# Two projections with the tokens on partitions, and their RMS norms taken on rows

## The chip, the core and the metric

The kernel runs on one core of one Trainium2 chip. The metric is the device time of one execution in microseconds (us), as the median of several executions. TensorE (PE) multiplies, with its weight loads shown apart (PEld); VectorE (DVE), ScalarE (ACT) and GpSimd (POOL) do the elementwise work; SyncE (SP) issues the loads of the weights from memory.

## The reference, cut to what matters

One sequence of 256 tokens, width 2048, passes a first block and then two more mixers. All is fp32. Of the first block this case is about what stands around w_o and w_down:

```python
def rms_norm(x, g):
    y = x * rsqrt(mean(x * x, axis=-1) + 1e-6)
    return y * g
m = concat([a, p]) @ w_o                      # 2048 x 2048
x = x + rms_norm(m, post_mix_g)
h = rms_norm(x, pre_ffn_g)
up = causal_dwconv(h @ w_up, conv_w, conv_b)  # 2048 x 11264, three taps
y = (gelu(up[..., :5632]) * up[..., 5632:]) @ w_down   # 5632 x 2048
x = x + rms_norm(y, post_ffn_g)
```

The second block begins with products of the token-shifted x: xs = x + (shift(x) - x) * mu, then xs @ a_w_in, a 2048 x 2048 matrix for each of four mu.

## The kernel before

**Precision.** Each fp32 operand is split in two fp32r parts: the high part is a rounded copy (ScalarE), the rest is the difference (VectorE). A product is high x high + rest x high + high x rest.

**Weights.** They come in units of 4 tiles of depth x 256 columns (3 tiles in the third w_down group), 512 KB each. SyncE loads unit u to raw slot u (RAWW, 8 slots) once the unit that held it is done (`unit_done`). ScalarE makes the high part in WHI, a ring of 4 slots (`split_unit`, L1620), once the unit four before it is done; VectorE makes the rest in WLO (L2330). `lo_made` then releases TensorE.

**Products.** In most of the kernel the weights are stationary and the tokens move (`unit`, L876): for each 128x128 weight tile one product with 512 columns (both parts of x, 256 tokens each) and one of the weight's rest with 256. A block is 512 output columns, 8 units, over the whole depth; its results lie with features on partitions, in four PSUM banks ACC. The other form stands in `token_rows` (L964) and `output_rows` (L1563): the tokens are stationary, the weights move, three products of 512 columns for each depth tile and token half, results with tokens on partitions. In the first block only the values and, at the end, w_out of the second mixer have that form.

**Order of the stretch.** w_in, attention and pooling; w_o (4 blocks); norm, residual, next norm's operand; then w_up and w_down in three groups of 16, 16 and 12 tiles of the inner width (GROUPS, L439): `tiles // 2` iterations of w_up, then 4 blocks of w_down whose sums are kept in Y; norm, residual, token shift; a_w_in.

**The norm between two products (before).** `scaled_norm_gemm` (L1005) runs w_o or the last w_down group. Pairs of tiles are evacuated to Y, squared by ScalarE (L1822), and scaled by the gain (L1826). Column sums of the squares are products with ones: `four_sums` within the product after units 15, 23 and 27, `token_sums` behind it; then root, reciprocal, `spread_column`, and filler products that keep TensorE at work (`keep_clock`, L890). `add_pair` (L2433) multiplies and adds two feature tiles to X; `h2_low` (L2561), or `mix_two` and `low_two` (L2677, L2686), make the next operand pair by pair. The next product starts with `first_body` (L901), in order of depth, which waits for the operand pair by pair. Its first 8 weight units are split during the norm (`split_ahead`), from places of their own (`raw_ahead`, L507).

**Order on each engine.** All programs are written out by hand, each engine in order, with semaphores between them.

## Time and profile before

| | us |
|---|---|
| median of 3 executions | 2172.55 (2169.7 to 2172.81) |
| profiled execution, its own time | 2170.59 |
| its span | 2168.8 |
| TensorE busy | 2140.4 (99%) |
| VectorE busy | 1487.4 (69%) |
| ScalarE busy | 1082.0 (50%) |
| mean granted TensorE clock | 0.994 |

The page gives one profiled execution. Busy shares are over the whole span. A matmul's duration in the timeline overlaps the next one's, so the pace of a product is read from start to start.

### The profile page before, as it was taken

How to read it: one execution, taken by the hardware profiler on the slowest of the kernel's cores; microseconds unless marked ns; L12 is line 12 of the kernel's file. 1: busy time of each engine (PE TensorE's matmuls, PEld its weight loads, DVE VectorE, ACT ScalarE, POOL GpSimd, SP SyncE). 2: the span in 40 equal slices, each digit the busy share in tenths (PEclk: the TensorE clock that was granted, in tenths of full speed). 3: DMA queues.
4: the chain of work that ended last, by engine and by line, in shares of the span. 5: the costliest groups of instructions: out<-in, count | busy, mean ns of one | idle time of the engine just before them, and what ended most of it. 6: DMA issues, size and time to landing. Idle time of an engine off the chain costs nothing.

```text
span 2168.8 us, 37737 instructions
## 1 busy us (share of the span) xinstructions
PE 2140.4 (99%) x14518; PEld 1832.7 (85%) x14518; DVE 1487.4 (69%) x2064; ACT 1082.0 (50%) x1529; POOL 85.8 (4%) x75
## 2 busy tenths in 40 slices
PE   9999999999999999999999999999899999999998
PEld 8888888888888888888788888887788888888886
DVE  6656568886488865886895589884676544567656
ACT  6444564444444443445654766544434534456543
POOL 0800000000000000000000000001211000000000
PEclk9999999999999999999999999999999999999999
DMA  9655545665666556555466666653454555654553
GB/s 301 210 160 164 167 146 184 185 192 186 191 186 190 187 190 188 187 183 175 151 189 192 185 180 181 204 169 83 132 166 150 184 184 194 185 155 146 172 197 116
DMA packets 398855, 384.42 MB, mean 177 GB/s; under 512 B 43660, under 2 KB 395460, under 8 KB 397764
## 3 DMA queue, kind: packets, MB, share of 16 engines
q1 hardware_dynamic: 398728, 382.66, 56.9%
q8 instruction: 88, 1.44, 0.3%
q14 instruction: 39, 0.32, 0.1%
HBM read 375.73 MB, written 6.87 MB: 176 GB/s over the span
## 4 chain that ended last, share of the span: by engine, by line
PE 91%; DVE 6%; issue 2%; ACT 1%; DMA 0%; POOL 0%; DVEq 0%; ACTq 0%; POOLq 0%
PE acc L884 44%; PE acc L887 22%; PE acc L915 4%; PE acc L977 2%; PE acc L978 2%; PE acc L979 2%; PE aux L1250 2%; PE acc L918 2%; PE acc L1550 1%; PE acc L1552 1%; PE acc L1551 1%; DVE w_lo L2805 1%; PE aux L1174 1%; DVE w_lo L2332 1%; DVE inverse L2796 0%
## 5 line engine op out<-in xcount | busy, mean ns | idle before, releaser
L2332 DVE TENSOR_TENSOR w_lo<-raw_w,w_hi 128x1024 fp32r<-128x1024 f32 (+1 forms) x576 | 693.6, 1224 | 429.0 <-ACT w_hi L1623 428.0
L1623 ACT ACTIVATE w_hi<-raw_w 128x1024 fp32r<-128x1024 f32 (+1 forms) x576 | 597.0, 1047 | 680.2 <-PE acc L887 541.2
L884 PE MATMUL acc<-h,w_hi 128*128 128x512 f32 x1664 | 525.7, 397 | 0.0
L887 PEld LDWEIGHTS acc<-h,w_lo 128*128 128x128 f32 x1664 | 312.6, 188 | 73.8
L887 PE MATMUL acc<-h,w_lo 128*128 128x256 f32 x1664 | 327.0, 278 | 0.0
L884 PEld LDWEIGHTS acc<-h,w_hi 128*128 128x128 f32 x1664 | 254.5, 189 | 0.8
L884 PE MATMUL acc<-x_split,w_hi 128*128 128x512 f32 x704 | 225.1, 401 | 0.0
L884 PE MATMUL acc<-ff,w_hi 128*128 128x512 f32 x704 | 221.5, 396 | 0.2 <-DVE w_lo L2332 0.2
L884 PE MATMUL acc<-xs_b,w_hi 128*128 128x512 f32 x512 | 162.0, 398 | 1.0 <-DVE w_lo L2805 0.9
L887 PEld LDWEIGHTS acc<-ff,w_lo 128*128 128x128 f32 x704 | 132.3, 188 | 31.3
L887 PEld LDWEIGHTS acc<-x_split,w_lo 128*128 128x128 f32 x704 | 132.2, 188 | 31.2
L2805 DVE TENSOR_TENSOR w_lo<-raw_w,w_hi 128x1024 fp32r<-128x1024 f32 x96 | 116.9, 1220 | 43.3 <-ACT w_hi L2055 42.4
L884 PE MATMUL acc<-xs_a,w_hi 128*128 128x512 f32 x448 | 142.2, 399 | 0.7 <-DVE w_lo L2805 0.7
L887 PE MATMUL acc<-x_split,w_lo 128*128 128x256 f32 x704 | 138.7, 278 | 0.0
L887 PE MATMUL acc<-ff,w_lo 128*128 128x256 f32 x704 | 138.3, 278 | 0.0
L2055 ACT ACTIVATE w_hi<-raw_w 128x1024 fp32r<-128x1024 f32 x96 | 100.7, 1054 | 54.5 <-PE acc L887 45.9
L887 PEld LDWEIGHTS acc<-xs_b,w_lo 128*128 128x128 f32 x512 | 96.2, 188 | 22.7
L884 PEld LDWEIGHTS acc<-x_split,w_hi 128*128 128x128 f32 x704 | 108.1, 189 | 2.5 <-issue 0.8
L884 PEld LDWEIGHTS acc<-ff,w_hi 128*128 128x128 f32 x704 | 107.1, 189 | 1.6 <-issue 0.8
L887 PEld LDWEIGHTS acc<-xs_a,w_lo 128*128 128x128 f32 x448 | 84.2, 188 | 19.9
L887 PE MATMUL acc<-xs_b,w_lo 128*128 128x256 f32 x512 | 100.6, 278 | 0.0
L1707 ACT ACTIVATE fold<-acc 128x512 f32<-128x512 f32 x128 | 74.8, 584 | 31.9 <-PE acc L887 21.8
(439 smaller groups left out, 3132.0 us busy)
## 6 DMA issues: line engine op xcount, KB each, us to landing
raw_w<-in_w_up SPq DMA_DIRECT2D x172, 512.0 KB, 3.5
raw_w<-in_a_w_in SPq DMA_DIRECT2D x124, 512.0 KB, 4.3
raw_w<-in_w_in SPq DMA_DIRECT2D x64, 512.0 KB, 4.0
raw_w<-in_w_down SPq DMA_DIRECT2D x64, 512.0 KB, 3.5
raw_w<-in_b_w_qg SPq DMA_DIRECT2D x64, 512.0 KB, 3.7
raw_w<-in_w_o SPq DMA_DIRECT2D x32, 512.0 KB, 3.5
raw_w<-in_a_w_out SPq DMA_DIRECT2D x32, 512.0 KB, 3.5
raw_w<-in_w_k_shared SPq DMA_DIRECT2D x32, 512.0 KB, 3.6
```

The costliest lines, as they stand in the source:

```text
L884: pe.matmul(ACC[2 * b + f], WHI[:, q if hi is None else hi, k, f * P:(f + 1) * P], op[:, kt, :, :].rearrange("p h t -> p (h t)"), start=fi ...
L887: mm = pe.matmul(ACC[2 * b + f][:, 0:T], WLO[:, slot, k, f * P:(f + 1) * P], op[:, kt, 0, :], start=False, stop=last)
L915: pe.matmul(ACC[2 * b + f], hi(2 * x + b)[:, k, f * P:(f + 1) * P], op[:, kt, :, :].rearrange("p h t -> p (h t)"), start=first, stop=False)
L918: mm = pe.matmul(ACC[2 * b + f][:, 0:T], lo(2 * x + b)[:, k, f * P:(f + 1) * P], op[:, kt, 0, :], start=False, stop=last)
L977: pe.matmul(out, xh, wh[:, :, k, :], start=(kt == 0), stop=False)
L978: pe.matmul(out, xh, wl[:, :, k, :], start=False, stop=False)
L979: mm = pe.matmul(out, xl, wh[:, :, k, :], start=False, stop=(kt == KD - 1))
L1623: act.activation(WHI[:, u % 4, 0:ku, :], RAWW[:, u, 0:ku, :], ACT.Copy).then_inc(hi_made, 1)
L1707: act.activation(FOLD[:, j0:j0 + 2, :], BANKS[:, j0:j0 + 2, T:], ACT.Copy, scale=scale).then_inc(low_half, 1)
L2055: act.activation(WHI[:, n % 4, :, :], RAWW[:, slot, :, :], ACT.Copy).then_inc(hi_made, 1)
L2332: dve.tensor_tensor(WLO[:, u, 0:ku, :], RAWW[:, u, 0:ku, :], WHI[:, u % 4, 0:ku, :].bitcast(F32), ALU.subtract)\
L2805: dve.tensor_tensor(WLO[:, slot_of(n), :, :], RAWW[:, slot_of(n), :, :], WHI[:, n % 4, :, :].bitcast(F32), ALU.subtract)\
```

## The change

w_o and w_down take the form with tokens stationary (`rows_block`), so Y holds token rows: half t_, piece c of 512 features. The squares are summed along a row by ScalarE's accumulator (`rows_squared`), the first three pieces' sums are added by VectorE (`first_squares`), and root, reciprocal and scaling act on a column of one number for each token. In the last block the last two quarters of depth run for token half 0 and then for half 1 (`last_rows_block`), so that half 0 is finished earlier. The scaled rows are turned back by TensorE (`rows_turned_back`) to features on partitions and added to X with the gain (`tile_added`). Half 0 and piece 0 of half 1 are turned behind the product; pieces 1 to 3 of half 1 within the next one, by `midway`, which `first_body` now calls behind the first two depth tiles of quarters 0, 1 and 2 (`if pr == 0 and b == 1 and x < 3`). The last two weight units of the product have high parts in HI2 (`split_last`), and the units split ahead have other places and turns: 0 to 3 before the norm, 4 between the halves, 5 to 7 between pairs. The core of the diff (indented less by eight columns; renamed semaphores and changed counts are left out):

```diff
-    ROOT2, RSTD2, AHEAD2 = (N2[1][:, 0, 0, 2 * k:2 * k + 2] for k in range(3))
+    ROOT2, RSTD2, AHEAD2, FIRST_SQUARES = (N2[1][:, 0, 0, 2 * k:2 * k + 2] for k in range(4))
+    SQUARE_SUMS = N2[1][:, 0, 0, 8:16].rearrange("p (t c) -> p t c", t=2)
+    ROWS = Y.rearrange("p (h a) t -> p h (a t)", h=2)
+    SQUARED = SQY.rearrange("p (h c a) t -> p h c (a t)", h=2, c=4)
...
 def hi_ahead(u):
-    return HI2[:, u] if u < 4 else WHI[:, u - 4]
+    return (HI2, HI2, WHI, WHI, WHI, WHI, HI2, HI2)[u][:, (2, 3, 2, 3, 0, 1, 0, 1)[u]]
...
+def hi_of_rows(x, last=False):
+    return HI2[:, 0:2] if last and x == 3 else WHI[:, 2 * x % 4:2 * x % 4 + 2]
...
+    for i in range(1, 4):
+        weights(1, lambda i_, b: (h["w_o"][0], i * 512 + b * 256), by_depth=512)
     for t0, tiles in GROUPS:
         weights(tiles // 2, lambda i, b: (w_up, i * 256 + (t0 * P + b * FF)), by_depth=256 if t0 == 0 else 0, ahead=0 if t0 == 0 else None)
-        late_depth_weights(lambda i, b: (w_down, b * 256), tiles // 4, t0)
-        weights(3, lambda i, b: (w_down, i * 512 + (512 + b * 256)), ku=tiles // 4, kt0=t0)
+        for i in range(4):
+            weights(1, lambda i_, b: (w_down, i * 512 + b * 256), ku=tiles // 4, kt0=t0, by_depth=512)
...
+                if pr == 0 and b == 1 and x < 3 and midway is not None:
+                    midway(x + 1)
...
-        keep_clock(6)
+    def depth_pass(op, out, x, q, k, ku, halves=(0, 1), last=False):
+        kt = q * ku + k
+        wh, wl = hi_of_rows(x, last)[:, :, k, :], WLO[:, 2 * x:2 * x + 2, k, :]
+        for t_ in halves:
+            xh, xl = (op[:, kt, part_, t_ * P:(t_ + 1) * P] for part_ in range(2))
+            pe.matmul(out[t_], xh, wh, start=(x + k == 0), stop=False)
+            pe.matmul(out[t_], xh, wl, start=False, stop=False)
+            mm = pe.matmul(out[t_], xl, wh, start=False, stop=(x == 3 and k == ku - 1))
+        return mm
+    def rows_block(op, i, ku=KU, depth=(0, 1, 2, 3), gate=None, after={}, quarters_done=4):
+        out = [ACC[2 * (i % 2) + t_] for t_ in range(2)]
+        for x in range(quarters_done):
+            pe.wait_ge(lo_made, seen(lo_made, 2))
+            if x == 0:
+                pe.wait_ge(acc_free, seen(acc_free, 2))
+            for k in range(ku):
+                if gate is not None:
+                    gate(depth[x], k)
+                mm = depth_pass(op, out, x, depth[x], k, ku)
+                if k == ku - 1:
+                    mm.then_inc(unit_done, 2)
+                if (x, k) in after:
+                    after[x, k]()
+        return out
+    def rows_turned_back(w, t_, c):
+        if c < 2:
+            pe.wait_ge(y_scaled, 4 * w + 2 * t_ + c + 1)
+        else:
+            pe.wait_ge(rows_scaled, 4 * w + 2 * t_ + c - 1)
+        if t_:
+            pe.wait_ge(row_pieces, 4 * w + c + 1)
+        for k in range(4):
+            mm = pe.transpose(AUX[c][:, k * P:(k + 1) * P], ROWS[:, t_, 512 * c + k * P:512 * c + (k + 1) * P], IDENT)
+        mm.then_inc(rows_turned, 1)
+    def last_rows_block(op, w, ku):
+        out = rows_block(op, 3, ku, quarters_done=2)
+        for t_ in range(2):
+            for x in (2, 3):
+                if t_ == 0:
+                    pe.wait_ge(lo_made, seen(lo_made, 2))
+                for k in range(ku):
+                    mm = depth_pass(op, out, x, x, k, ku, halves=(t_,), last=True)
+                    if t_ and k == ku - 1:
+                        mm.then_inc(unit_done, 2)
+            if t_ == 0:
+                mm.then_inc(half_done, 1)
+        for c in range(4):
+            rows_turned_back(w, 0, c)
+        keep_clock(1)
+        rows_turned_back(w, 1, 0)
+        seen(sq_ready, 8)
     def post_norm_gemm(op, first, bufs):
...
         pe.wait_ge(lo_made, seen(lo_made))
         unit(A1, n // 4 % 2, n % 4, n % 8)
         beside_unit(n)
-    scaled_norm_gemm(B1, lambda: first_body(B1, [(pool_mix_ready, 8)] * 4 + [(mix_ready, 2 * n + 2) for n in range(4)], depth=DEPTH_W_O,
-                                            after={n: (lambda n=n: beside_unit(32 + n)) for n in range(8)}))
-
+    def mix_gate(q, k):
...
+    for i in (1, 2):
+        rows_block(B1, i)
+    last_rows_block(B1, 0, KU)
+    pe.sem_inc(acc_free, 2)
-    first_body(A2, pairs_of(operand), after={5: x2_sums, 6: lambda: gather(AUX[0], N2[2])}, hi=hi_ahead, lo=lambda u: lo_ahead(0, u))
+    first_body(A2, pairs_of(operand), after={5: x2_sums, 6: lambda: gather(AUX[0], N2[2])}, hi=hi_ahead, lo=lambda u: lo_ahead(0, u),
+               midway=lambda c: rows_turned_back(0, 1, c))
     for n, (t0, tiles) in enumerate(GROUPS):
         gemm(tiles // 2 - (n == 0), A2, [])
+        ku = tiles // 4
+        gated_quarters = quarters(gated_ready, ku)
+        def ff_gate(q, k):
+            if k == 0:
+                pe.wait_ge(*gated_quarters[q])
...
+            rows_block(B2, i, ku)
         if n < len(GROUPS) - 1:
-            late_depth_body(B2, quarters(gated_ready, tiles // 4), tiles // 4)
-            gemm(3, B2, [], ku=tiles // 4)
...
+            rows_block(B2, 3, ku)
+    last_rows_block(B2, 1, ku)
...
-    def squared(i, j0):
-        act.wait_ge(acc_free, seen(acc_free, 0, "tile"))
...
+        act.activation(HI2[:, u - 6, 0:ku, :], RAWW[:, u, 0:ku, :], ACT.Copy).then_inc(hi_made, 1)
+    def rows_squared(i, t_, src):
+        act.activation(SQUARED[:, t_, i, :], src, ACT.Square, accum_out=SQUARE_SUMS[:, t_, i:i + 1]).then_inc(sq_ready, 1)
         seen(sq_ready)
+    def rows_of_block(i, copied=None):
+        act.wait_ge(unit_done, seen(unit_done, 8, "tile"))
+        seen(acc_free, 2, "tile")
+        for t_ in range(2):
+            if copied is None:
+                rows_squared(i, t_, ACC[2 * (i % 2) + t_])
+            else:
+                copied(i, t_)
+    def half_norm(w, t_, squared_last, last_piece):
+        if t_ == 0:
+            act.wait_ge(half_done, w + 1)
+        else:
+            act.wait_ge(unit_done, seen(unit_done, 8, "tile"))
+        squared_last(t_)
+        if t_ == 0:
+            act.wait_ge(var_ready, seen(var_ready))
         act.wait_ge(sq_ready, seen(sq_ready, 0))
-        for k in range(2):
-            kt = 4 * i + j0 + k
...
+        act.activation(ROOT2[:, t_:t_ + 1], SQUARE_SUMS[:, t_, 3:4], ACT.Sqrt, scale=1.0 / D,
+                       bias=FIRST_SQUARES[:, t_:t_ + 1]).then_inc(rstd_ready, 1)
+        act.wait_ge(columns_ready, 2 * w + t_ + 1)
+        for c in (2, 3):
+            act.activation(y_row(t_, c), last_piece(t_) if c == 3 else y_row(t_, c), ACT.Copy,
+                           scale=RSTD2[:, t_:t_ + 1]).then_inc(rows_scaled, 1)
+    def blocks_in_rows(ku, evac, first=1):
+        for i in range(first, 4):
+            for u in range(8):
+                if u == 3:
+                    evac(i - 1)
+                if (i, u) == (3, 4):
+                    act.activation(AHEAD2, ONES[:, 0:2], ACT.Sqrt)
+                if i == 3 and u >= 6:
+                    split_last(u, ku)
+                else:
+                    split_unit(u, ku)
+    blocks_in_rows(KU, rows_of_block)
+    for u in range(4):
+        split_ahead(0, u)
+    for t_ in range(2):
+        if t_:
+            split_ahead(0, 4)
+        half_norm(0, t_, lambda t_: rows_squared(3, t_, ACC[2 + t_]), lambda t_: ACC[2 + t_])
+    seen(acc_free, 2, "tile")
     def x_squared(j):
...
+        if p_ in (2, 4, 6):
+            split_ahead(0, 4 + p_ // 2)
...
+            act.wait_ge(acc_free, seen.total(acc_free, "tile") - 1 + t_)
+            rows_squared(i, t_, y_row(t_, i))
+    def last_sum_squared(t_):
+        act.wait_ge(acc_free, seen(acc_free, 1, "tile"))
+        rows_squared(3, t_, y_row(t_, 3))
     pend = None
     for n, (t0, tiles) in enumerate(GROUPS):
...
+        split(0, ku)
+        pend(lambda: two_splits(4, ku))
+        two_splits(6, ku)
+        evac = (lambda i: rows_of_block(i, copied_rows), rows_left, squared_sums)[n]
+        if n < len(GROUPS) - 1:
+            for i in range(1, 4):
+                for u in range(8):
+                    if u == 3:
+                        evac(i - 1)
+                    split_unit(u, ku)
+            pend = lambda evac=evac: evac(3)
+        else:
+            blocks_in_rows(ku, evac)
+    for u in range(4):
+        split_ahead(1, u)
+    for t_ in range(2):
+        if t_:
+            split_ahead(1, 4)
+        half_norm(1, t_, last_sum_squared, lambda t_: y_row(t_, 3))
     def silu_out(dst):
...
+            if p_ in (3, 5, 7):
+                split_ahead(1, 5 + (p_ - 3) // 2)
...
-
-        y2, x2 = Y[:, 2 * p_:2 * p_ + 2, :], X[:, 2 * p_:2 * p_ + 2, :]
...
+    def split_last(u, ku=KU):
+        dve.wait_ge(hi_made, seen(hi_made))
+        dve.tensor_tensor(WLO[:, u, 0:ku, :], RAWW[:, u, 0:ku, :], HI2[:, u - 6, 0:ku, :].bitcast(F32), ALU.subtract).then_inc(lo_made, 1)
+    def blocks_in_rows(ku, evac, last=True):
+        for i in range(1, 4):
+            for u in range(8):
+                if u == 3:
+                    evac(i - 1)
+                if last and i == 3 and u >= 6:
+                    split_last(u, ku)
+                else:
+                    split_unit(u, ku)
+    def first_squares(sums):
+        dve.wait_ge(sq_ready, sums)
+        link(dve.tensor_reduce(FIRST_SQUARES, SQUARE_SUMS[:, :, 0:3], AX.X, ALU.add))
+        dve.tensor_scalar(FIRST_SQUARES, FIRST_SQUARES, 1.0 / D, NORM_EPS, ALU.mult, ALU.add).then_inc(var_ready, 1)
+    def half_scaled(w, t_):
+        dve.wait_ge(rstd_ready, seen(rstd_ready))
+        dve.reciprocal(RSTD2[:, t_:t_ + 1], ROOT2[:, t_:t_ + 1]).then_inc(columns_ready, 1)
+        dve.wait_ge(columns_ready, 2 * w + t_ + 1)
+        for c in range(2):
+            dve.tensor_scalar(y_row(t_, c), y_row(t_, c), RSTD2[:, t_:t_ + 1], None, ALU.mult).then_inc(y_scaled, 1)
+    def tile_added(kt, t_, gain):
+        g, now = COL[gain] + kt, slice(t_ * P, (t_ + 1) * P)
+        return dve.scalar_tensor_tensor(X[:, kt, now], AUX[kt // 4][:, kt % 4 * P:(kt % 4 + 1) * P], PV[:, g:g + 1], X[:, kt, now],
+                                        ALU.mult, ALU.add)
+    def first_half_added(w, c, gain):
+        dve.wait_ge(rows_turned, 8 * w + c + 1)
+        for k in range(4):
+            ins = tile_added(4 * c + k, 0, gain)
+        ins.then_inc(row_pieces, 1)
+    def pair_added(w, p_, gain):
+        if p_ % 2 == 1 and p_ < 6:
+            first_half_added(w, (p_ + 1) // 2, gain)
+        if p_ % 2 == 0:
+            dve.wait_ge(rows_turned, 8 * w + 4 + p_ // 2 + 1)
+        for k in range(2):
+            ins = tile_added(2 * p_ + k, 1, gain)
+        ins.then_inc(x_ready, 1)
...
-        seen(part_out)
-        split_ahead(which, last)
...
+    def copied_rows(i):
+        seen(unit_done, 8, "tile")
+        for t_ in range(2):
+            dve.wait_ge(sq_ready, 4 + 2 * i + t_ + 1)
+            dve.tensor_copy(y_row(t_, i), ACC[2 * (i % 2) + t_]).then_inc(acc_free, 1)
+        seen(acc_free, 2, "tile")
+        if i == 2:
+            first_squares(4 + 6)
+    blocks_in_rows(KU, copied_rows)
+    seen(unit_done, 8, "tile")
+    for u in range(4):
+        split_ahead(0, u)
+    dve.wait_ge(acc_free, seen(acc_free, 0, "tile"))
+    half_scaled(0, 0)
+    first_half_added(0, 0, "post_mix_g")
+    half_scaled(0, 1)
+    seen(acc_free, 2, "tile")
...
             h2_low(p_ - 1)
-        if p_ == 5:
-            split_ahead(0, 7)
+        if p_ in (1, 4, 6, 8):
+            split_ahead(0, (1, 4, 6, 8).index(p_) + 4)
     partial(AUX[0], N2[2])
...
+    def last_half_sum(t_):
+        if t_ == 0:
+            dve.wait_ge(half_done, 1 + 1)
...
+        else:
+            dve.wait_ge(unit_done, seen(unit_done, 8, "tile"))
+        dve.tensor_tensor(y_row(t_, 3), ACC[2 + t_], y_row(t_, 3), ALU.add).then_inc(acc_free, 1)
+        dve.wait_ge(acc_free, seen(acc_free, 1, "tile"))
     pend = None
     for n, (t0, tiles) in enumerate(GROUPS):
         pend = gemm(tiles // 2, up_evac(t0), pending=pend, keep=True, by_depth=(n == 0), early=2 * (n == 0))
-        pend = gemm(4, joiner(Y) if n == 0 else adder(), pending=pend, ku=tiles // 4, keep=True, by_depth=True)
-    first_groups()
-    last_pair_and_reciprocal(1, (0, 1, 2, 3), (4,), 5)
+        ku = tiles // 4
+        split(0, ku)
+        pend(lambda: two_splits(4, ku))
+        two_splits(6, ku)
+        evac = (rows_of_act, summed_rows, last_sums)[n]
+        blocks_in_rows(ku, evac, last=(n == 2))
+        pend = lambda evac=evac: evac(3)
+    for u in range(4):
+        split_ahead(1, u)
+    last_half_sum(0)
+    half_scaled(1, 0)
+    last_half_sum(1)
+    first_half_added(1, 0, "post_ffn_g")
+    half_scaled(1, 1)
     def shift_diff(i):
...
-        if p_ < 8:
-            add_pair(p_)
         if p_ >= 2:
             low_two(p_ - 2)
+        if p_ < 8:
+            pair_added(1, p_, "post_ffn_g")
         if 1 <= p_ < 9:
             dve.wait_ge(x_ready, 8 + p_)
             mix_two(p_ - 1)
-        if p_ in (5, 7):
-            split_ahead(1, {5: 6, 7: 7}[p_])
+        if p_ in (1, 4, 6, 8):
...
```

## Rows read from the trace of the kernel before

**Rows 1.** The page, part 1: busy us, share and instructions of the engines.

```profile
PE 2140.4 (99%) x14518; PEld 1832.7 (85%) x14518; DVE 1487.4 (69%) x2064; ACT 1082.0 (50%) x1529; POOL 85.8 (4%) x75
```

**Rows 2.** Waits of TensorE, 470 to 1066 us: total, times, longest.

```profile
PE aux L994 <- ACT sq L1824: 0.5, 1, 0.5
...
PE acc L884 <- DVE w_lo L2332: 0.2, 1, 0.2
```

**Rows 3.** TensorE's timeline (start, us, engine line op), 1080 to 1094 us.

```profile
1080.72 0.63 PE L915 MATMUL acc<-xs_a,w_hi 128*128 128x512 f32 x2
...
1091.87 0.63 PE L884 MATMUL acc<-xs_a,w_hi 128*128 128x512 f32 x2
```

**Rows 4.** The chain that ended last (start, us, what), in the last product.

```profile
2069.40 0.87 PE aux L1560 x8
...
2137.38 0.87 PE aux L1560 x8
```

**Rows 5.** The same chain, in the first product: sums of four groups.

```profile
27.74 1.86 PE aux L956 x32
```

**Rows 6.** ScalarE by form, 1000 to 1034 us: count, busy us, mean ns, idle.

```profile
L1623 ACT ACTIVATE w_hi<-raw_w 128x768 fp32r<-128x768 f32 x14 | 11.0, 833 | 2.8 <-PE acc L887 2.8
...
L1824 ACT ACTIVATE sq<-y 128x512 f32<-128x512 f32 x5 | 3.2, 632 | 13.2 <-DVE y L2629 13.2
```

**Rows 7.** By form: VectorE, 1000 to 1034 us; ScalarE's accumulator read, 140 to 220.

```profile
L2332 DVE TENSOR_TENSOR w_lo<-raw_w,w_hi 128x768 fp32r<-128x768 f32 x15 | 13.7, 955 | 13.0 <-ACT w_hi L1623 13.0
L2629 DVE TENSOR_TENSOR y<-acc,y 128x512 f32<-128x512 f32 x3 | 2.1, 692 | 0.3
...
L1786 ACT ACTIVATION_READ_ACCUMULATOR scores<-scores,softmax_stats 128x1 f32 x16 | 3.0, 187 | 0.0
```

**Rows 8.** TensorE's timeline around the norm behind w_o.

```profile
304.77 0.40 PE L887 MATMUL acc<-mix,w_lo 128*128 128x256 f32 x2
...
314.76 0.87 PE L915 MATMUL acc<-h,w_hi_ahead 128*128 128x512 f32 x2
...
339.82 0.63 PE L884 MATMUL acc<-h,w_hi 128*128 128x512 f32 x2
```

**Rows 9.** VectorE by form, 140 to 220 us: an operation of 128 columns on PSUM.

```profile
L2503 DVE SCALAR_TENSOR_TENSOR scores<-aux,rstd_columns,bias 128x128 f32<-128x128 f32 x8 | 2.8, 347 | 0.3 <-PE aux L1100 0.3
```

**Rows 10.** VectorE's timeline in both boundaries: rest of h2, mix, weight split ahead.

```profile
315.01 0.87 DVE L2566 SCALAR_TENSOR_TENSOR h<-x,params,h 128x256 fp32r<-128x256 f32 x2
...
322.15 1.22 DVE L2338 TENSOR_TENSOR w_lo_ahead_b<-raw_w_ahead_b,w_hi 128x1024 fp32r<-128x1024 f32 x1
...
1066.68 0.88 DVE L2682 SCALAR_TENSOR_TENSOR xs_quarter<-x,params,xs_quarter 128x255 f32<-128x255 f32 x2
```

**Rows 11.** TensorE's timeline around the norm behind w_down.

```profile
1056.00 0.50 PE L994 MATMUL aux<-consts,ms 128*128 128x1 f32 x4
...
1066.82 1.22 PE L915 MATMUL acc<-xs_a,w_hi_ahead 128*128 128x512 f32 x2 [3.18 <-DVE xs_a L2688]
```

**Rows 12.** Timelines there of SyncE's issues and of ScalarE.

```profile
1047.06 0.37 SPq L593 DMA_DIRECT2D raw_w<-in_a_w_in  x1
...
1054.33 1.06 ACT L1628 ACTIVATE w_hi_ahead<-raw_w 128x1024 fp32r<-128x1024 f32 x1 [1.41 <-DMA raw_w<-in_a_w_in]
```

**Rows 13.** Timelines there of ScalarE's copy and VectorE's rest of one pair.

```profile
1064.90 0.61 ACT L1938 ACTIVATE xs_a<-xs_quarter 128x512 fp32r<-128x512 f32 x1
...
1066.08 0.69 DVE L2688 TENSOR_TENSOR xs_a<-xs_quarter,xs_a 128x512 fp32r<-128x512 f32 x1
```

**Rows 14.** Stretches: us, then busy us and count of PE, PEld, DVE, ACT, POOL; granted clock; DMA.

```profile
308.00:315.00 7.00, 6.54 (x21) 5.45 (x20) 5.94 (x10) 4.87 (x10) 0.00 (x0) 0.51 0.01 2
...
1063.60:1066.80 3.20, 0.04 (x1) 0.00 (x0) 3.17 (x7) 2.10 (x6) 0.00 (x0) 0.85 0.00 0
1066.80:1072.30 5.50, 5.48 (x17) 4.71 (x18) 5.43 (x11) 3.15 (x7) 0.00 (x0) 0.50 0.01 3
1072.30:1080.00 7.70, 7.70 (x45) 6.67 (x44) 7.63 (x14) 3.74 (x8) 0.00 (x0) 0.98 0.45 136
```

189 lines of the change are left out of this document (61 added, 128 removed).

## The prediction

> **What bounds the kernel now.** I read the page's busy times first: TensorE is busy 2140.4 of 2168.8 us [rows 1], so only time on TensorE, or a wait of TensorE, can move the end. Then the waits of TensorE over the whole feed-forward block: half a microsecond for the sums, 0.2 us for a weight rest [rows 2]; the w_down products run back to back and VectorE and ScalarE are hidden. What remains is (a) the pace of the products, (b) the two stretches in which a norm stands between two products, and (c) what a slower VectorE or ScalarE would newly expose. I take them in this order, against the profiled execution (2170.6 us, span 2168.8). It lies 2 us under the median of 2172.55, inside the spread of the three runs; I do not correct for that.
>
> **(a) Pace of the products.** The kernel already holds both forms. With weights stationary, eight depth tiles of a 512-column block take 1080.72 to 1091.87, 11.15 us, 1.394 us each [rows 3]. With tokens stationary (the last product, w_out of the second mixer) the turned pieces of X come at 2069.40 and 2137.38, three blocks of 16 tiles later [rows 4]: 22.66 us a block, less 0.87 for the eight transposes is 21.79, or 1.362 us a tile. Both stream 3072 columns a tile; eight products become six. Gain 0.032 us a tile. w_o has 64 tiles, w_down 4 x (16 + 16 + 12) = 176, together 240: **-7.6 us**. The squares no longer have their sums taken inside the product: 3 groups in each of the two products, 1.86 us for four such groups [rows 5], so 6 x 0.465 = **-2.8 us**. The order of depth at the start of w_down and of w_o asks for the last quarter at three quarters of the block in both kernels, and the last conv pair and its split end before that, so I cost that at nothing (cover: some 4 us; without it the wait is the overrun itself).
>
> The Trainium skill, "TensorE: Matmul & The Clock Gate", section on the 53.3 and 56 ns, gives about 2.5 ns of fixed cost per matmul when warm. Two products fewer would by that be worth 5 ns a tile, 1.2 us in all instead of 7.6, and the forecast would be 6.4 us later. The two rows speak against it here: they give about 14 ns for each product saved.
>
> **(b) The new chain between evacuation and the next weight split.** In blocks 1 to 3 ScalarE and VectorE split weight unit 2, evacuate the block before, then split unit 3, which TensorE wants one quarter into the block: 5.45 us with 4 tiles a unit, 4.09 us with 3. Unit 2 can't be split before the block starts, since its slot is read until then. With 4 tiles: high part of unit 2 to 1.1 us, evacuation (at worst two squares with their accumulator reads) to 2.5, high part of unit 3 to 3.5, rest to 4.8 us: hidden, 0.6 us to spare. In the third w_down group (3 tiles) the order is high part (0.83), rest (0.96), sums on VectorE (0.69 each), squares of the sums on ScalarE (0.63 plus 0.19 for the accumulator), high part, rest [rows 6, 7]. Added with overlap: rest of unit 2 ends at 1.9, sums at 2.5 and 3.2, squares at 3.35 and 4.05, high part of unit 3 starts there, its rest starts at 4.9 and ends at 5.9. TensorE wants it at 4.1. Wait 1.8 us, three times: **+5.5 us** (bounds 0, if the squares slip behind, and 6). Queued behind the squares on ScalarE is the high part of unit 3, and TensorE waits for its rest.
>
> **(c1) Boundary w_o to w_up.** Now the last w_o product ends at about 305.0, the first behind the norm starts at 314.76, and the next loop at 339.82: 34.8 us [rows 8]. After the change, in us from the end of w_o: the first token half is normed by -0.6 (it ended 5.45 us earlier). TensorE turns its four pieces to 1.8. VectorE adds four tiles of the first piece: a 128x128 scalar-tensor-tensor out of PSUM takes 0.347 [rows 9], back to back about 0.27, so 1.15 us, to 1.8. The second half: square to 1.1, root 1.35, reciprocal 2.0, first piece scaled 2.5, turned 3.3, pair added 3.9, then the other half's second piece and the next pair to 5.6 (1.15 + 0.6), rest of h2 (0.87) to 6.5 [rows 10]. First product at 6.6 instead of 9.8: -3.2. But then the pieces turned inside the product make a loop of two engines: TensorE works two depth tiles (2.79 us), turns piece c of the second half, and its *next* gate is an operand pair that VectorE computes only behind the addition which waits for that turn. So TensorE stands for: landing 0.3, two tiles 0.6, rest 0.87, signal 0.1 = 1.85 us. This happens three times (c = 1, 2, 3), plus 0.9 once where four first-half tiles also fall in, plus 0.95 for the sum of squares of x, whose last square comes later: +7.4. The transposes are 3 x 0.45 = 1.35. TensorE reaches the next loop at 40.0 instead of 34.8: **+5.2 us**.
>
> **(c2) Boundary w_down to a_w_in.** Now 1056.0 to 1066.82, and 1091.87 to the next loop: 35.9 us [rows 3, 11]. Here the raw weights come late already: the fourth landed only at 1054.33, 7.3 us behind its issue [rows 12]. The change frees raw slots 2 and 3 at half of the last block, 8.2 us before its end; at the pace of rows 12 the fourth lands at about -1.5 and is split before half 0 is normed. Then: rest of the fourth +0.7, sum 1.4, square 2.2, scaled 3.5; second half sum 4.1, square 5.5, scaled 6.4, turned 7.2, pair 7.8, second piece and pair 9.5, mix (0.87) 10.4, split ahead (1.22) 11.6, rest (0.69) 12.25 [rows 10, 13]: first product at 12.35 instead of 10.8. Inside the product the loop is longer, because between the addition and the gate lie the mix (0.87), ScalarE's copy (0.61) and the rest (0.69): landing 0.3, tiles 0.6, 0.9, 0.7, 0.7 = 3.25 us at c = 1, and at c = 2 and 3 a weight split (1.22) covers the copy's 0.7 and adds 0.5: 3.75 each. Between them 1.25, 1.2 and 1.3 where the first-half tiles or the last pair are late. Sum of waits 14.6, transposes 1.35. Next loop at 50.7, at full clock, instead of 35.9: **+14.8 us**. Every moved step was counted: four tile adds per piece, two per pair, the splits ahead at 1, 4, 6, 8, and SP's order (0, 1, 4, 2, 5, 3, 6, 7), in which 2 and everything behind it waits for the half block.
>
> **Clock.** In both boundaries the granted clock is at the lower level (1.2 GHz) for some microseconds: 0.51 over 308 to 315, and 0.50 over 1066.8 to 1072.3 after 3.2 us without work; 17 matmuls passed in those 5.5 us, against 45 in the 7.7 us behind them [rows 14]: 3.1 a microsecond against 5.8. The change has fewer filler products (1 for 8) and five stretches of 3 us and more without a product. Bounds: nothing, and lower clock through both products (2.35 us on each of some six to eight pairs of tiles, about +16). I take the first pair of (c2) at the lower clock, +2.35, and 1.1 us behind each of its three long waits, since the pair behind a wait has 1.25 us of slack: **+5.7 us**.
>
> Sum: -7.6 - 2.8 + 5.5 + 5.2 + 14.8 + 5.7 = +20.8, so 2170.6 + 20.8 = **2191.4 us**.
>
> **Rivals.**
> A, the other side (faster): VectorE is not in TensorE's way, because additions run ahead and the gate behind a turned piece is already met. For it: VectorE now needs about 2.1 to 2.7 us a pair against 2.79 of TensorE [rows 10]. Against: in the program's order the rest of pair 1 stands behind the addition of pair 2, which waits for the turn. It decides if that wait costs under about 1 us each. Then: -7.6 - 2.8 - 3.2 + 1.35 + 1.5 + 1.35 = -9.4, or 2161 us (2167 with the wait of (b)).
> B: only (c2) is real; (b) hides and (c1)'s loop is half as long: -10.4 + 2 + 14.8 + 2.4 = +8.8, 2179 us.
> C, the clock: the short stretches of work between waits never bring the higher clock back. Price +16 instead of +5.7: 2202 us. For it: the clock is low after a pause half as long as what I expect. Against: the products of the second mixer's end keep theirs. The Trainium skill, "TensorE: Matmul & The Clock Gate", says in its section on the HAM clock gate that the lower clock is the default and activity releases it. Rows 14 agree as far as they go.
> D: a product saved is worth next to nothing, so that only the columns count and (a) shrinks from 7.6 to 1.2 us: 2198 us. For it: both forms stream 3072 columns a tile. Against: the two rows of (a). It is the rule of the Trainium skill weighed in (a).
>
> **How the numbers follow.** Forecast 0.62, A 0.10, B 0.12, C 0.13, D 0.03. The range 2174 to 2205 takes in B, C, D and the bounds of (b) and of the clock, and leaves out A and a little at the top. About 0.2% (4.3 us) is what a measurement of this kernel can tell from no change. Slower by more: the forecast, C, D and most of B, 0.83; within: the edges of A and B, 0.08; faster: 0.09.
>
> **What the changed profile would show.** (a) w_down blocks of 21.8 us (4 tiles) without waits. (b) three waits of TensorE of about 1.8 us on a weight rest in the third group. (c1) first h2 product 6 to 7 us behind w_o, then waits for the operand h of 1.85 us. (c2) waits for xs_a of 3 to 4 us, three of them, and a lower clock around them. What would make it wrong: waits of TensorE in the two first products under 5 us together, or a block that takes 22.3 us as before.

## The result, and the profile after

| | before | after |
|---|---|---|
| median, us | 2171.63 (2169.7 to 2172.81, 4 executions) | 2195.46 (2193.83 to 2196.85, 4 executions) |
| ratio to before, 95% interval | | 1.0112 (1.0100 to 1.0124) |
| profiled execution, its own time, us | 2170.59 | 2193.83 |
| its span, us | 2168.8 | 2192.1 |

The kernel is 1.1% slower. The forecast was 2191.4 us, in the range 2174 to 2205, and against the profiled execution it said +20.8 us where +23.2 came. How much of that agreement is the sum of right terms, and how much is errors that cancel, is what the rest of this document takes apart.

First the page's busy times of the kernel after, beside [rows 1]:

```profile
PE 2135.0 (97%) x13978; PEld 1813.1 (83%) x13978; DVE 1467.8 (67%) x2082; ACT 1064.0 (49%) x1515; POOL 85.8 (4%) x75
```

TensorE is busy 5.4 us less than before, in a span that is 23.3 us longer. The change did save TensorE work; what it costs is waits and, behind them, time at the lower clock. So the next view is the waits of TensorE (engine, line, what it waited for; us in total, times, longest us) from 200 us to the start of the loop behind the second boundary. They add up to 33 us (the four largest are shown). In the kernel before the same stretch has under 6 us, 3.2 of them one wait for xs_a behind w_down [rows 11], and the feed-forward block has 0.7 us [rows 2]:

```profile
PE acc L920 <- DVE xs_a L2857: 14.1, 4, 4.8
PE acc L920 <- DVE h L2708: 7.9, 5, 3.0
PE aux L1042 <- DVE y L2558: 5.1, 2, 4.4
PE acc L1011 <- DVE w_lo L2430: 5.0, 4, 1.6
```

L920 is the high product inside `first_body`, L1042 the turning of a row piece, L1011 the first product of a depth pass in the rows form. Cut by the places where one stage hands over to the next, the two profiled executions compare like this (each mark is the start of the first product of the stage, or the end of the last):

| stretch, us | before | after | difference | forecast |
|---|---|---|---|---|
| to the end of w_o | 305.00 | 299.75 | -5.25 | -3.4 |
| w_o's end to the next loop | 34.8 | 41.05 | +6.25 | +5.2 |
| from there to w_down's end | 716.2 | 713.9 | -2.3 | -1.5 |
| w_down's end to a_w_in's next loop | 35.9 | 57.0 | +21.1 | +20.5 |
| the rest | 1076.9 | 1080.4 | +3.4 | 0 |
| sum | 2168.8 | 2192.1 | +23.3 | +20.8 |

**(a) The pace.** Timeline of TensorE inside a w_down block (start, duration, engine, line, operation, tiles; the pace is start to start). Eight depth passes, one for each token half of four depth tiles, lie between the two rows:

```profile
820.05 0.39 PE L1011 MATMUL acc<-w_hi,ff 128*128 128x512 f32 x1
...
825.49 0.39 PE L1011 MATMUL acc<-w_hi,ff 128*128 128x512 f32 x1
```

5.44 us for four tiles is 1.360 a tile, against 1.394 with weights stationary [rows 3]. Granted clock 1.00 in both kernels from 340 to 1054 us, so the difference is not the clock.

**(b) The third group.** Two of the waits of the third w_down group; there is one in each of its four blocks, of 0.21, 1.61, 1.61 and 1.60 us:

```profile
991.59 0.50 PE L1011 MATMUL acc<-w_hi,ff 128*128 128x512 f32 x1 [0.21 <-DVE w_lo L2430]
...
1005.74 0.50 PE L1011 MATMUL acc<-w_hi,ff 128*128 128x512 f32 x1 [1.61 <-DVE w_lo L2430]
```

What the wait at 1005.74 ended with is in VectorE's timeline: the rest of that unit, which itself waited for its high part. ScalarE began that part at 1003.86, when the second square was done:

```profile
1004.72 2.70 DVE L2430 TENSOR_TENSOR w_lo<-raw_w,w_hi 128x768 fp32r<-128x768 f32 x3 [1.54 <-ACT w_hi L1678]
```

**(c1) The boundary behind w_o.** The timeline of TensorE, with the waits in brackets [us idle <- who ended it]; the turns (transposes of row pieces) are L1042, the first product of the next loop is L889:

```profile
299.75 1.91 PE L1042 MATMUL aux<-consts,y 128*128 128x128 f32 x16
...
306.49 0.73 PE L920 MATMUL acc<-h,w_hi_ahead 128*128 128x512 f32 x2 [3.04 <-DVE h L2708]
...
313.03 0.74 PE L920 MATMUL acc<-h,w_hi_ahead 128*128 128x512 f32 x2 [1.49 <-DVE h L2708]
...
318.73 0.60 PE L1042 MATMUL aux<-consts,y 128*128 128x128 f32 x4
320.82 0.73 PE L920 MATMUL acc<-h,w_hi 128*128 128x512 f32 x2 [1.49 <-DVE h L2708]
...
324.30 0.73 PE L920 MATMUL acc<-h,w_hi 128*128 128x512 f32 x2 [0.41 <-DVE h L2708]
...
329.29 0.74 PE L920 MATMUL acc<-h,w_hi 128*128 128x512 f32 x2 [1.49 <-DVE h L2708]
...
332.83 1.93 PE L956 MATMUL aux<-sq,consts 128*32 128x256 f32 x32 [0.47 <-ACT sq L1937]
...
340.80 0.63 PE L889 MATMUL acc<-h,w_hi 128*128 128x512 f32 x2
```

The first product starts 6.7 us behind the end of w_o (forecast 6.6, before 9.8 [rows 8]). Behind each turn inside the product stands a wait of 1.49 us for the operand h: four tiles turned at 318.73, done at 319.33, and nothing until 320.82.

**(c2) The boundary behind w_down.** The same view, with the three turns inside the product (1074.58, 1085.55, 1097.87):

```profile
1059.14 3.67 PE L1042 MATMUL aux<-consts,y 128*128 128x128 f32 x16 [4.40 <-DVE y L2558]
...
1063.46 1.06 PE L1042 MATMUL aux<-consts,y 128*128 128x128 f32 x4
1069.30 1.22 PE L920 MATMUL acc<-xs_a,w_hi_ahead 128*128 128x512 f32 x2 [4.78 <-DVE xs_a L2857]
...
1074.58 0.85 PE L1042 MATMUL aux<-consts,y 128*128 128x128 f32 x4
1078.31 1.08 PE L920 MATMUL acc<-xs_a,w_hi_ahead 128*128 128x512 f32 x2 [2.89 <-DVE xs_a L2857]
...
1085.55 0.60 PE L1042 MATMUL aux<-consts,y 128*128 128x128 f32 x4
1089.37 1.22 PE L920 MATMUL acc<-xs_a,w_hi 128*128 128x512 f32 x2 [3.23 <-DVE xs_a L2857]
...
1097.87 0.60 PE L1042 MATMUL aux<-consts,y 128*128 128x128 f32 x4
1101.70 0.73 PE L920 MATMUL acc<-xs_a,w_hi 128*128 128x512 f32 x2 [3.23 <-DVE xs_a L2857]
...
1111.73 0.63 PE L889 MATMUL acc<-xs_a,w_hi 128*128 128x512 f32 x2
```

The 16 turns of the first half start 4.40 us late, at 1059.14; w_down ended at 1054.74. The first product starts 14.6 us behind that (forecast 12.35, before 10.8 [rows 11]). Then 2.89, 3.23 and 3.23 us of wait behind the three turns. Who held the first pieces up stands in two rows of ScalarE's timeline and the first two of VectorE's; the third is its first addition of the second half:

```profile
1054.18 1.06 ACT L1683 ACTIVATE w_hi<-raw_w 128x1024 fp32r<-128x1024 f32 x1 [3.01 <-DMA raw_w<-in_a_w_in]
1057.19 0.63 ACT L1884 ACTIVATE sq<-y 128x512 f32<-128x512 f32 x1 [1.95 <-DVE y L2788]
```
```profile
1055.27 1.22 DVE L2436 TENSOR_TENSOR w_lo<-raw_w,w_hi 128x1024 fp32r<-128x1024 f32 x1 [2.84 <-ACT w_hi L1683]
1056.41 0.68 DVE L2788 TENSOR_TENSOR y<-acc,y 128x512 f32<-128x512 f32 x1
...
1064.56 2.16 DVE L2563 SCALAR_TENSOR_TENSOR x<-aux,params,x 128x128 f32<-128x128 f32 x8 [1.62 <-PE aux L1042]
```

The fourth weight unit of a_w_in was issued at 1047.59 and landed 6.6 us later. ScalarE stood 3.01 us for it, VectorE 2.84 us for ScalarE, and the sum of the first token half (L2788), whose products had ended at 1050.6, stood queued behind it until 1056.41. The second half's first piece was turned at 1063.46, and VectorE added from 1064.56 on.

**The clock.** Windows of the kernel after, from w_down's end to the first product and from there to the next loop (us, busy and instructions of each engine, granted clock, DMA):

```profile
core 0: us, PE busy (x) PEld busy (x) DVE busy (x) ACT busy (x) POOL busy (x), PEclk, DMA share, GB/s
1054.70:1069.30 14.60, 5.42 (x24) 4.69 (x23) 10.33 (x25) 8.41 (x17) 0.00 (x0) 0.73 0.05 16
1069.30:1111.70 42.40, 33.06 (x140) 27.98 (x141) 23.63 (x50) 15.48 (x26) 0.00 (x0) 0.77 0.26 85
```

Before, the whole boundary had a granted clock of 0.90; here it is 0.73 and 0.77, TensorE at its lower level (1.2 GHz) for about half of the time.

### The profile page after: what moved, and what is told of

It is laid out like the page before. It is cut to its first block, busy times and chain, and to the rows that moved or that the text cites. A ratio compares the mean times of both kernels' runs of the same rounds, so it can differ in the third digit from the quotient of the medians.

```text
span 2192.1 us, 36112 instructions
## 1 busy us (share of the span) xinstructions
PE 2135.0 (97%) x13978; PEld 1813.1 (83%) x13978; DVE 1467.8 (67%) x2082; ACT 1064.0 (49%) x1515; POOL 85.8 (4%) x75
## 4 chain that ended last, share of the span: by engine, by line
PE 87%; DVE 8%; ACT 2%; issue 2%; DMA 1%; POOL 0%; SPq 0%; DVEq 0%; ACTq 0%; POOLq 0%
PE acc L889 34%; PE acc L892 17%; PE acc L1011 4%; PE acc L1013 4%; PE acc L1012 4%; PE acc L920 3%; PE acc L977 2%; PE acc L979 2%; PE acc L978 2%; PE aux L1305 2%; PE acc L923 1%; DVE w_lo L2974 1%; PE acc L1605 1%; PE acc L1607 1%; PE acc L1606 1%
## 5 line engine op out<-in xcount | busy, mean ns | idle before, releaser
L1678 ACT ACTIVATE w_hi<-raw_w 128x1024 fp32r<-128x1024 f32 (+1 forms) x572 | 588.9, 1046 | 711.2 <-PE acc L892 412.9
L889 PE MATMUL acc<-h,w_hi 128*128 128x512 f32 x1664 | 525.7, 397 | 0.0
L889 PEld LDWEIGHTS acc<-h,w_hi 128*128 128x128 f32 x1664 | 254.7, 189 | 1.0
L889 PE MATMUL acc<-x_split,w_hi 128*128 128x512 f32 x704 | 225.1, 401 | 0.0
L889 PE MATMUL acc<-xs_b,w_hi 128*128 128x512 f32 x512 | 162.1, 398 | 2.0 <-DVE w_lo L2974 2.0
L889 PE MATMUL acc<-xs_a,w_hi 128*128 128x512 f32 x448 | 142.2, 399 | 0.7 <-DVE w_lo L2974 0.7
L1011 PE MATMUL acc<-w_hi,ff 128*128 128x512 f32 x346 | 135.1, 390 | 5.0 <-DVE w_lo L2430 5.0
L1012 PE MATMUL acc<-w_lo,ff 128*128 128x512 f32 x352 | 137.0, 389 | 0.0
L1013 PE MATMUL acc<-w_hi,ff 128*128 128x512 f32 x346 | 134.6, 389 | 0.0
L889 PEld LDWEIGHTS acc<-x_split,w_hi 128*128 128x128 f32 x704 | 108.2, 189 | 2.4 <-issue 0.8
L892 PE MATMUL acc<-xs_a,w_lo 128*128 128x256 f32 x448 | 88.1, 278 | 0.0
L889 PEld LDWEIGHTS acc<-xs_b,w_hi 128*128 128x128 f32 x512 | 78.0, 189 | 4.6 <-DVE w_lo L2974 2.6
```

What stands on the lines that cost most here:

```text
L889: pe.matmul(ACC[2 * b + f], WHI[:, q if hi is None else hi, k, f * P:(f + 1) * P], op[:, kt, :, :].rearrange("p h t -> p (h t)"), start=fi ...
L892: mm = pe.matmul(ACC[2 * b + f][:, 0:T], WLO[:, slot, k, f * P:(f + 1) * P], op[:, kt, 0, :], start=False, stop=last)
L1011: pe.matmul(out[t_], xh, wh, start=(x + k == 0), stop=False)
L1012: pe.matmul(out[t_], xh, wl, start=False, stop=False)
L1013: mm = pe.matmul(out[t_], xl, wh, start=False, stop=(x == 3 and k == ku - 1))
L1678: act.activation(WHI[:, u % 4, 0:ku, :], RAWW[:, u, 0:ku, :], ACT.Copy).then_inc(hi_made, 1)
```

## The experiments

Two of the theories are told apart by edits of order alone. The loop theory: TensorE's waits inside the first products come from where VectorE's program puts the rest of an operand, and from where the turns stand. Against it: VectorE's load (no order helps), the clock, and the late transfer. Times are compared as ratios to the kernel before on the same chip; stretches are read from the traces.

| kernel | median, us | ratio to before (95%) | w_o's end to next loop | w_down's end to next loop |
|---|---|---|---|---|
| before | 2171.63 | | 34.8 | 35.9 |
| after | 2195.46 | 1.0112 (1.0100 to 1.0124) | 41.1 | 57.0 |
| after, again | 2192.02 | 1.0092 (1.0077 to 1.0107) | 41.9 | 56.2 |
| rests first | 2185.85 | 1.0065 (1.0047 to 1.0082) | 38.3 | 52.8 |
| unit 3 first | 2189.72 | 1.0079 (1.0063 to 1.0096) | | 55.6 |
| norm ahead of unit 4 | 2190.01 | 1.0078 (1.0061 to 1.0095) | | 53.8 |
| eight products | 2200.35 | 1.0124 (1.0106 to 1.0142) | | |
| 12 fillers | 2196.63 | 1.0110 (1.0094 to 1.0125) | | 57.0 |
| 5 fillers | 2192.53 | 1.0095 (1.0080 to 1.0111) | | 52.3 |
| pipelined | 2175.05 | 1.0014 (1.0005 to 1.0023) | 35.6 | 43.3 |
| combined | 2165.15 | 0.9968 (0.9958 to 0.9979) | 33.6 | 40.4 |
| combined, with two steps more | 2166.65 | 0.9973 (0.9964 to 0.9982) | 32.1 | 41.8 |

The kernel after was run twice; its ratios differ by 0.2%, so a single ratio is not trusted here to better than that. The finer readings come from the traces. There the waits that follow from the order of the program have the same length to 0.03 us from run to run (1.49; 2.89, 3.23, 3.23). The wait for the first pieces behind w_down, which hangs on a transfer, does not: 3.6 to 5.1 us in the seven traces with the order of the kernel after at that place. Boundaries that an edit does not touch differ too: the first takes 41.1 to 42.7 us, the second 55.6 to 57.0. So a difference of up to 1.7 us in a whole boundary says nothing by itself.

### The rest of an operand ahead of the addition that waits

```diff
+                if p_ % 2 == 0 and p_ >= 2:
+                    h2_low(p_ - 1)
                 if p_ < 8:
                     pair_added(0, p_, "post_mix_g")
-                if p_ >= 1:
+                if p_ % 2 == 1:
                     h2_low(p_ - 1)
...
```

The second boundary likewise: mix and rest of the odd pair ahead of the even pair's addition, and ScalarE's copies in that order.

> VectorE takes the rest of the odd pair (h2, xs_a) ahead of the addition that waits for the turned piece, in both first products; ScalarE's copies of xs_a follow the same order. Loop theory (the program's order on VectorE makes TensorE wait behind each turned piece): the waits for h (1.49 us three times, 0.41, 0.47 in the kernel after) go below 1 us together, those for xs_a inside the product (2.89, 3.23, 3.23) below 3 us together, since VectorE has 6.4 us of work for every 6.0 us of TensorE there; with the clock held up the time falls by 10 to 17 us from 2195.5, to 2178 to 2186. Rival, VectorE's throughput (it has too much work in these stretches whatever the order): the waits move to the pairs ahead of the turned pieces and keep at least two thirds of their 14.7 us; 2190 to 2196.

Measured: ratio 1.0065, profiled 2185.48 us against 2193.83, in the upper part of the loop theory's range. Its timeline of TensorE in the first boundary:

```profile
311.10 0.60 PE L1042 MATMUL aux<-consts,y 128*128 128x128 f32 x4
311.46 0.71 PE L920 MATMUL acc<-h,w_hi_ahead 128*128 128x512 f32 x2
...
314.74 0.73 PE L920 MATMUL acc<-h,w_hi 128*128 128x512 f32 x2 [0.24 <-DVE h L2713]
...
322.42 0.73 PE L920 MATMUL acc<-h,w_hi 128*128 128x512 f32 x2 [1.37 <-DVE h L2713]
...
330.25 1.93 PE L956 MATMUL aux<-sq,consts 128*32 128x256 f32 x32 [1.54 <-ACT sq L1937]
```

The product behind the turn at 311.10 now starts at 311.46 with no bracket: the three waits of 1.49 us are gone, as the loop theory says. But one pair further on there are new ones, 0.24 and 1.37 us, and 1.54 at the squares. In the second boundary the same: nothing behind the turns, then 1.98, 3.11 and 2.09 us a pair later, where 9.35 us had stood before; 7.2 are left, three quarters, against under 3 expected. Of the 14.7 us of waits 10.3 are left, 70%, which is what the rival said (at least two thirds); the time, 2185.9, is what the loop theory said. So this run did not decide between the two. What it shows is that the first link was real, since the waits behind the turns are gone; the new ones suggested a second link that still hung on the turn: the next even pair cannot be added before its piece is turned, and TensorE turned it only halfway through. The next run tests that.

### Turns one pair earlier, VectorE in step

```diff
                 for x, q in enumerate(depth):
+                    if midway is not None and x < 3:
+                        pe.wait_ge(*gates[2 * x])
+                        midway(x + 1)
...
-                        if pr == 0 and b == 1 and x < 3 and midway is not None:
-                            midway(x + 1)
...
+            for c in range(4):
+                pair_added(0, 2 * c, "post_mix_g")
+                h2_low(2 * c)
+                pair_added(0, 2 * c + 1, "post_mix_g")
+                split_ahead(0, 4 + c)
+                h2_low(2 * c + 1)
...
```

The old loop over the pairs goes. `pair_added` of an even pair now also adds the first half's next piece, so that its bank is free one pair earlier. The second boundary has the same order, with the mixes between, and ScalarE rounds a pair before it scales the next.

> Each piece of the second token half is turned one pair earlier (as soon as the pair before is there), and VectorE goes in step: addition of the even pair, first half of the next piece, rest of the even pair, then the odd pair; in the second boundary ScalarE rounds each pair before it scales the next. Loop theory, refined by the run with the rests first (removing the wait behind the turn left waits of 0.2, 1.4, 1.5 us for h and 2.0, 3.1, 2.1 us for xs_a, since the next addition still hung on the turn): with both links cut the waits inside the first h2 product go below 0.7 us together and those inside the first xs_a product below 3 us; w_o's end to the next loop 34.7 us instead of 41.0, w_down's end to the next loop 46 instead of 57; 2178 us. Rival (VectorE's work of about 27 us between w_down's end and the next loop is the bound whatever the order): the second boundary stays above 52 us, 2184 to 2187 us.

Measured: 2175.05 us, ratio 1.0014; boundaries 35.6 and 43.3 us (34.7 and 46 expected). Once it has begun, the first h2 product has no wait left. The first xs_a product has two, 0.70 and 2.08, where 9.35 us had been:

```profile
1061.51 1.12 PE L1043 MATMUL aux<-consts,y 128*128 128x128 f32 x4 [3.94 <-DVE xs_a L2855]
...
1083.08 0.74 PE L923 MATMUL acc<-xs_a,w_hi_ahead 128*128 128x512 f32 x2 [0.70 <-DVE xs_a L2855]
...
1086.82 1.19 PE L923 MATMUL acc<-xs_a,w_hi_ahead 128*128 128x512 f32 x2 [2.08 <-DVE xs_a L2855]
```

This is the main result, and here the rival (the second boundary above 52 us) is out. Of a loss of 20 to 24 us (by the two ratios of the kernel after), 17 to 21 were the order of instructions on VectorE, ScalarE and TensorE: the same instructions in another order take 19.2 us out of the two boundaries (5.5 and 13.7), counted against the first trace of the kernel after. That includes the time at the lower clock that stood behind the waits.

### The unit that TensorE wants first, ahead of the evacuation

```diff
-            def blocks_in_rows(ku, evac, last=True):
+            def blocks_in_rows(ku, evac, last=True, at=3):
...
-                        if u == 3:
+                        if u == at:
                             evac(i - 1)
...
-                blocks_in_rows(ku, evac, last=(n == 2))
+                blocks_in_rows(ku, evac, last=(n == 2), at=3 + (n == 2))
```

ScalarE's program has the same edit.

> In the third w_down group the weight unit that TensorE wants a quarter into the block is split ahead of the evacuation, its sums and squares. Theory (chain through sums and squares): the 5.0 us that TensorE waits for w_lo in that group go to under 0.5, 2190.5 us. Rival (the two engines have too much work in a block of three-tile units): the wait moves to the next unit, and 2 to 5 us stay; 2192.5 to 2195.5.

Measured: ratio 1.0079. Waits for w_lo in that group 1.0 us in two, not 5.0 in four. The last block keeps a wait, at half its former length:

```profile
1042.73 0.50 PE L1011 MATMUL acc<-w_hi,ff 128*128 128x512 f32 x1 [0.78 <-DVE w_lo L2430]
```

That is not under 0.5 us, as expected, but 4.0 of the 5.0 us go, and the rival would have kept at least 2. So the evacuation ahead of unit 3 was the cause; that it acted through the squares is what the rows of (b) show. The boundaries of this run are within the spread of untouched ones.

### The norm ahead of the late unit

```diff
-            for u in range(4):
+            for u in range(3):
                 split_ahead(1, u)
             last_half_sum(0)
             half_scaled(1, 0)
+            split_ahead(1, 3)
             last_half_sum(1)
```

On ScalarE units 3 and 4 stand behind the norm of the first half.

> Behind w_down the fourth weight unit, which lands late, is split behind the norm of the first token half instead of ahead of it. Theory (the late transfer holds up the first half's norm, that the second's, and that the first product behind it): the wait of 4.4 us for the first turned pieces disappears, the first xs_a product starts about 3.6 us earlier behind the end of w_down (11.1 instead of 14.7 us), 2192 us, or 2190 if less time at the lower clock follows. Rival (the second half's chain sets the first product anyway, the 4.4 us are slack): under 1 us, 2195 us.

```profile
1056.50 1.97 PE L1042 MATMUL aux<-consts,y 128*128 128x128 f32 x16 [0.59 <-DVE y L2559]
...
1062.01 0.66 PE L1042 MATMUL aux<-consts,y 128*128 128x128 f32 x4 [3.11 <-DVE y L2559]
1067.44 1.22 PE L920 MATMUL acc<-xs_a,w_hi_ahead 128*128 128x512 f32 x2 [4.78 <-DVE xs_a L2859]
```

w_down ended at 1055.91: the first pieces are there 0.59 us later instead of 4.40, and the first product starts 11.5 us behind the end instead of 14.6. Against this one trace of the kernel after the late transfer cost 3.0 us, 3.6 were expected; against the 13.5 to 15.1 us of all seven traces with the old order it is 2.0 to 3.6. Part of what it gave (3.11 us) is now the wait for the second half's first piece, since unit 3 and unit 4 stand in front of that half's square on ScalarE.

### Eight products of the same columns

```diff
-                    pe.matmul(out[t_], xh, wl, start=False, stop=False)
+                    for f in range(2):
+                        pe.matmul(out[t_][:, f * UNIT_COLS:(f + 1) * UNIT_COLS], xh, wl[:, f, :], start=False, stop=False)
```

> The middle one of the three products of a depth tile and token half is issued as two products of 256 columns, so that w_o and w_down have again eight products for each depth tile, of the same 3072 columns. Theory (a product saved is worth 16 ns, by which the rows of 1.394 and 1.362 us differ): 480 products more cost 7.6 us, blocks of w_down with 4-tile units take 22.3 us, 2203 us. Rival (the columns alone count, and a product costs 2.5 ns, as the Trainium skill has it in TensorE: Matmul & The Clock Gate, the gain came from the operands' roles): +1.2 us, 2196.7 us, blocks of 21.8 us.

```profile
819.81 0.39 PE L1011 MATMUL acc<-w_hi,ff 128*128 128x512 f32 x1
...
825.39 0.39 PE L1011 MATMUL acc<-w_hi,ff 128*128 128x512 f32 x1
```

Eight passes take 5.58 us, 1.395 a tile, against 5.44 and 1.360. Two products more, same columns, same operand roles: 0.035 us a tile, 17 ns a product, and the pace is that of the kernel before (1.394). w_o ends at 302.15 instead of 299.75, 2.4 us for 64 tiles. The span is 6.9 us longer. The timed ratio, 1.0124 against 1.0112 and 1.0092, goes the same way; its intervals alone would not decide between 1.2 and 7.6 us. Each product here comes with a load of its own weights, so the run does not say how much of the 17 ns is the product and how much the load. The Trainium skill, "TensorE: Matmul & The Clock Gate", section "Wait — 56ns, not 53.3ns?", has about 2.5 ns of fixed cost for a warm product; the trace does not agree for these fp32r products that each load their own weights.

### Fillers in the waits

```diff
+            def turned_and_filled(c):
+
+                rows_turned_back(1, 1, c)
+                for _ in range(12):
+                    pe.matmul(AUX[c - 1][:, 0:T], ONES, CF[:, 0:T], start=True, stop=True)
```

> Twelve small products of 256 columns (1.3 us at the higher clock, 2.6 us at the lower one) follow each of the three turns inside the a_w_in product and fill the waits of 2.9, 3.2 and 3.2 us that TensorE has there; they write to a bank that is free. Clock theory (the low level in this stretch comes from TensorE standing still, and the product loses some 6.7 us to it): the granted clock stays up for part of the product and 2 to 4 us come back, 2192 us. Rival (the lower level here has another cause, or the fillers are too few to matter): no change within 1 us, 2195.5 us; if the fillers at the lower level outlast a wait, up to 1 us is lost.

Measured: no gain, 1.0110, and the boundary takes 57.0 us as before the edit. By the expectation that speaks for the rival. The timeline says otherwise:

```profile
1078.00 5.34 PE L1049 MATMUL aux<-consts 128*128 128x256 f32 x24
1083.00 0.81 PE L920 MATMUL acc<-xs_a,w_hi_ahead 128*128 128x512 f32 x2
```
```profile
1072.00:1083.00 11.00, 10.98 (x45) 9.61 (x45) 4.08 (x13) 1.84 (x4) 0.00 (x0) 0.73 0.01 1
1083.00:1114.00 31.00, 31.00 (x171) 27.25 (x170) 19.76 (x38) 13.66 (x23) 0.00 (x0) 1.00 0.36 113
```

Twelve fillers took 5.0 us, not 1.3: each is two instructions of 0.21. They outlasted the waits of 2.89, 3.23 and 3.23 by 5.7 us together. That the boundary still took 57.0 means that 6 us came back, and the granted clock is 1.00 from 1083 on, where it was 0.77. So the run could not tell the two apart by its time, and it was made again with five:

> As the run with twelve fillers, with five behind each turn. There a filler took 0.42 us, not the 0.11 that its columns suggested (two instructions each), so twelve took 5.0 us and outlasted waits of about 3; the granted clock was 1.00 from the second turn on. Five take 2.1 us. Clock theory (the low level behind the waits is worth about 6 us, and work in the waits gives it back): w_down's end to the next loop 51 to 52 us instead of 57.0, 2189 us. Rival (a waiting product has to be covered whole, or the fillers' gain was an accident of where the low stretches fell): 55 us and more, 2193 to 2196 us.

```profile
1070.10:1109.00 38.90, 33.86 (x171) 28.11 (x171) 23.30 (x50) 15.50 (x26) 0.00 (x0) 0.95 0.30 92
```

That row is the product's stretch, with the columns of the windows above.

52.3 us, and 0.95 in the product. The three waits behind the turns are 0.73, 1.07 and 1.07 us with 2.1 us of fillers in front, and three of 0.7 to 0.8 us appear between them, where the lower clock had hidden VectorE's pace. Of the 4.7 us that the boundary is shorter, 1.1 lie ahead of the first product, where no filler stands (13.5 us instead of 14.6). The product itself takes 38.8 us instead of 42.4: 3.6 us are what five fillers give back, in a trace. The timed ratio (1.0095) lies between the two of the kernel after and shows no gain that I could vouch for.

### Combined, and one step too far

The pipelined order, unit 3 ahead, the norm ahead of the late unit, and ScalarE's fifth unit behind the second half's norm in both boundaries:

> The pipelined order, with the weight unit a quarter into the blocks of the third group split ahead of the evacuation, and both norms ahead of the late weight splits (fourth unit of a_w_in on VectorE behind the second half's scaling, fifth unit of both on ScalarE behind the second half's norm). If the three causes found so far (order on VectorE, chain through the squares, late transfer ahead of the norm) are all, their gains add: first h2 product about 5 us behind w_o, first xs_a product 7 to 8 us behind w_down, the boundaries 33 and 41 us, w_down without waits; 2166 us (2163 to 2171), 0.1 to 0.4% under the kernel before. Rival (the lower clock and VectorE's load take back what the order gives): 2172 to 2180, not under the kernel before.

Measured: 2165.15 us, ratio 0.9968 (0.9958 to 0.9979): 0.3% under the kernel before, so both kernels are beaten. The boundaries are 33.6 and 40.4 us, and the gains did add. The first xs_a product starts only 11.4 us behind w_down, not 7 to 8: the *third* unit was late now, and held the sum up for 3.2 us, as the fourth had done. The last run takes that away too, moves ScalarE's fifth unit of a_w_in in among the pairs, and puts fillers into both gaps (against the combined kernel; only VectorE's and TensorE's part is shown):

```diff
-            for u in range(3):
+            for u in range(2):
                 split_ahead(1, u)
             last_half_sum(0)
             half_scaled(1, 0)
+            split_ahead(1, 2)
             last_half_sum(1)
...
                 rows_turned_back(w, 1, 0)
+                keep_clock((4, 6)[w])
```

> The combined kernel with two more steps in the second boundary: the norm of the first token half ahead of the third weight unit too (in the combined kernel that unit landed 3.2 us late and held the sum up), and fillers behind the turn in the gaps of both boundaries (four and six, 1.7 and 2.6 us, in waits of 2.8 and 4.6). Theory: the wait of 1.9 us for the first pieces and that of 1.05 us for the second half's first piece go, and the low clock in the second boundary is shorter: w_down's end to the next loop 37 us instead of 40.4, 2162 us (2160 to 2164). Rival (VectorE's 27 us of work between the two loops set the end of this stretch, so that an earlier first product only lengthens the waits behind it): 40 us, 2165 us as before.

```profile
1041.50:1083.30 41.80, 32.65 (x175) 27.08 (x174) 34.75 (x74) 23.03 (x39) 0.00 (x0) 0.96 0.32 99
```
```profile
1042.60:1083.00 40.40, 29.32 (x163) 24.68 (x162) 33.09 (x74) 24.66 (x43) 0.00 (x0) 0.92 0.32 99
```

The rival holds: the second boundary takes 41.8 us, not 37, though the first product starts 1.4 us earlier and the clock is higher, 0.96 for 0.92. The saved time turned up as seven waits for xs_a, 5.1 us together, where the combined kernel has four of 3.5 us, and as lower clock behind the last and longest of them (2.08 us). The run makes two changes at once, so it does not say what each of them did. VectorE is busy 34.75 of 41.8 us (33.09 of 40.4 in the combined kernel); the kernel before had 33.46 of 35.9. (The 27 us that two expectations give for VectorE's work are too low.) With 33 us and more of work on VectorE, another order alone cannot bring this stretch much under the 35.9 of the kernel before; this is argued from the busy times and was not tried. About seven us of the stretch lie above VectorE's own work; how much of them is its load, unevenly spread, and how much the chain over ScalarE (two crossings for each pair) was not told apart.

> The kernel after, unchanged, beside the others on the same chip, so that their times are compared with its own there: 2195.5 us, ratio to the kernel before 1.011.

Measured: 2192.02 us, ratio 1.0092. The second trace shows the same waits as the first (1.49 three times; 2.89, 3.23, 3.23) with the late transfer at 3.62 instead of 4.40 us.

## Why the prediction was right, step by step

**(a) Pace: right, and its cause shown.** The prediction's rows give 16 ns for each product saved (0.032 us over two products); the "about 14 ns" in its text does not follow from them. -0.034 us a tile measured, -0.032 forecast; w_down's stretch with its waits of 5.0 us taken out is 7.3 us shorter, 7.0 were forecast for pace and sums together. w_o gave 5.25 instead of 3.4. In the kernel before, eight tiles and one sum took 11.92 us there (from the sum at 281.26 to that at 293.18), 0.3 us more than 8 x 1.394 + 0.465: a sum costs more than its own duration [rows 5]. Three of them make 0.9 of the missing 1.9 us; the rest stays open. The eight-product run shows that it is the number of products that counts. Rival D, by which a product saved is worth next to nothing, is out.

**(b) Right, a little too dear.** 1.61, 1.61 and 1.60 us for the three forecast waits of 1.8, plus 0.21 at the group's first block: 5.0 against 5.5. The chain named (sums, then squares, then the high part of unit 3) was the cause, as the rows above and the run with unit 3 first show. The small wait at the first block was not in the sum.

**(c1) The first product right to 0.1 us, the loop right in kind.** The forecast waits were 1.85 three times, 0.9 and 0.95; measured 1.49 three times, 0.41 and 0.47. The term was 7.4 and should have been 5.4. In exchange the first products ran at the lower clock, for which I had put nothing at this place: the first two depth tiles took 4.45 us (306.49 to 310.94) instead of 2.79, 1.7 us more. The three turns took 1.8 us instead of 1.35. And the written term is itself smaller than its parts: -3.2 + 7.4 + 1.35 is +5.55, not +5.2. That the sum is only 1 us off is luck: errors of 2 us each way cancel.

**(c2) Right in sum by luck, wrong in its parts.** Its terms, and what they measured:
- First product at 12.35 us: 14.6. The landing of the fourth unit was put at 1.5 us ahead of the end; 8.2 us of lead and 7.3 us from issue to landing [rows 12] give 0.9, and it came 0.6 ahead. That carried through to the second half, whose first piece was scaled at about 7.8 us instead of 6.4. The rest of the 2.2 us is the clock, for which nothing was put here: behind a wait of 4.40 us the 16 turns took 3.67 us, against 1.91 behind w_o, so that the second half's piece was turned later and VectorE began to add at 9.8 us instead of 7.2. That the split stands ahead of the norm was in the prediction's chain; the run with the norm first shows what this order costs.
- Waits of 3.25, 3.75 and 3.75 behind the turns: 2.89, 3.23 and 3.23.
- Waits between them of 1.25, 1.2 and 1.3: none. At the lower clock TensorE's pair takes longer than VectorE's, so the clock hid them; in the run with five fillers, at a granted clock of 0.95, three of 0.7 to 0.8 us are there. The term was 14.6 and measured 9.35. The three turns took 2.05 us instead of 1.35.
- The clock, +5.7 (2.35 for the first pair of tiles, 1.1 behind each of three waits): from turn to turn the product takes 5.28, 7.24, 8.50 and 10.03 us, less the turns and waits in them; at full pace these 2, 4, 4 and 6 tiles would take 2.79, 5.58, 5.58 and 8.36. So the first pair lost 2.5 us, and the tiles behind the three waits 1.7, 2.9 and 1.7, together 8.7. The first pair was right; behind the waits 3.3 became 6.3. This is the term that was mis-sized most. The kernel before has the 2.5 us of the first pair too, so against it the product lost 6.2 us more by the clock. The first filler run gave about 6 us back, the second 3.6.

So in (c2) the first product came 2.2 us later and the waits were 5.3 us shorter than forecast, the clock cost 3.1 us more and the turns 0.7: together 0.7 us, and the term looks right. In the two first products the lower clock cost 10.4 us, where the sum had 5.7.

**The two rivals that could have bent it.** A (VectorE runs ahead and nothing waits) was wrong for this program. The pipelined run meets its condition in the first h2 product, but not in the first xs_a product (2.8 us of waits), and measures 2175 us where A said 2161 or 2167; the combined kernel is at 2165, with edits that A does not have. C, the clock at its dearest, has 10.4 us measured, about halfway between the 5.7 forecast and the 16 feared. Its condition, that the higher clock never comes back between the waits, did not hold: from 1082.06 on the steps are 0.70 us again. What it shares with the forecast, that the waits bring the lower clock, is confirmed: where fillers cover the waits, the granted clock is 1.00. B (only the second boundary is real) falls with the +6.25 us of the first.

**The rest, +3.4 us, was not in the sum.** The windows of the two kernels around the layer norm's boundary, before and then after (columns as above):

```profile
1600.00:1690.00 90.00, 89.75 (x545) 76.34 (x544) 59.27 (x71) 43.02 (x56) 5.43 (x4) 0.98 0.49 155
```
```profile
1620.00:1713.00 93.00, 92.59 (x552) 79.03 (x552) 60.65 (x73) 43.28 (x55) 5.44 (x4) 0.96 0.46 154
```

0.98 against 0.96 of granted clock over the same work, and another 1.1 us are waits for w_lo in the woven stage (2.7 against 1.6). In the traces of the other kernels this rest, which no edit touches, is between 1078.6 and 1082.7 us, so it differs by some 4 us from execution to execution. The waits for w_lo vary as well: 1.6 us, as before, in the runs with the rests first and pipelined. But all eleven traces with the new form lie above the 1076.9 of the kernel before, by 1.7 to 5.8 us. With one trace of the kernel before, it stays open how much of the 3.4 us is this variation and how much the change.

## What to carry to other kernels

When an engine's program interleaves two chains, look for the instruction that waits for the other engine and ask what stands behind it: here a rest that was computable stood behind an addition that was not, and most of the loss came from such orders. Put work that depends on a late transfer behind the chain that sets the gap, never ahead of it; taking one late unit out of the way showed the next. And when a wait is removed, look one step further before you count the gain: the first reordering took 6.9 us out of the two boundaries, the second 19.2, because the wait had a second link.

## What the runs showed of the hardware that was not expected

- The same 3072 columns take 1.395 us in eight products and 1.360 in six, at a granted clock of 1.00: 17 ns for a product more.
- An fp32 filler of 256 columns is two instructions and takes 0.42 us at the granted clock of 1.00 (twelve in 5.0 us), four times what its columns at the fp32r pace (512 in 0.227 us) would suggest.
- A wait of 3 us inside a product cost its own length and then two thirds as much again: behind 9.35 us of waits (2.89, 3.23, 3.23) the tiles took 6.3 us more than at full pace, and 2.1 us of products put into each wait brought the granted clock of the stretch from 0.77 to 0.95. Behind the waits of 1.49 us in the first boundary the steps are 0.70 us, full pace; behind one of 2.08 us in the last run some are 1.28.
